# One loop over all 32 experts, and a 4 MB stage for the next expert's down blocks, copied home by GpSimd

## The chip, the core and the metric

The kernel runs on one core of a Trainium2 chip. The metric is the device time of one execution in microseconds; the median of three runs of the kernel before is 1277.75 us. TensorE (PE) multiplies, VectorE (DVE), ScalarE (ACT) and GpSimd (POOL) do the rest, and SyncE (SP) issues the large transfers from HBM.

## The reference, cut to what matters

One layer of a streaming encoder over 320 tokens (256 of a prompt, 64 of a sample), width 1024, in fp32: modulation, a combined projection, stick-breaking attention beside an mLSTM, an output projection, and then a mixture of experts. Only the last part is touched by the change:

```python
logits = h @ w_router + b_router            # h (320, 1024), 32 experts
top_val, top_idx = lax.top_k(logits, 4)
gates = softmax(top_val)
# for each expert e, over the tokens that chose it:
gu = h[tok] @ w_gu[e] + b_gu[e]             # (1024, 2048)
x_glu, x_lin = split(gu); x_glu = min(x_glu, 7); x_lin = clip(x_lin, -7, 7)
act = x_glu * sigmoid(1.702 * x_glu) * (x_lin + 1)
acc[tok] += (act @ w_down[e] + b_down[e]) * gate   # (1024, 1024)
x = x + ga2 * acc
```

Each expert has 8 MB of `w_gu` and 4 MB of `w_down`, so 32 experts are 384 MB that cross from HBM once.

## The kernel before, in words

**Memory.** `ring` has 12 units of 1 MB (128 partitions x 2048 fp32). Before the experts it holds chunks of `w_ada`, `w_in` and `w_out`; then units 0 to 7 hold the eight row blocks of an expert's `w_gu` and units 8 to 11 the four blocks of its `w_down`. `work` is a scratch area that the stages share: first attention and mLSTM, then, from its start on, the expert stage (`h2p`, the tokens in three bf16 parts; `xg`, `actT`, `gc`, `lc`, `sg`, `otok`, `spread`, `pick`, `wpick`, and so on).

**Transfers.** SP issues all weight transfers in program order. The twelve units of expert 0 are issued as the last chunks of `w_ada` and `w_out` are used (L500 to L502). Then a loop over experts 1 to 31 (L509) calls `load_expert`: unit j of expert e waits until PE has used unit j of expert e - 1 (`gu_used` for j below 8, `dn_used` for the others), in the order 0 to 11. After the loop SP stores the output when DVE's last additions are done (`acc_ready`).

**An expert on PE** (`expert`, L1004): read three token counts (this expert's, the one's before, the one's after); wait for `xg`; the bias and blocks 0 to 2 of gate/up (`gate_up`, L907, or L897 and L900 for one size); the first half of the scatter of the expert before (`scatter`, L978); blocks 3 to 5; the second half of that scatter; blocks 6 and 7 and the transposition of the gate weights (`turn_pick`, L968); the gather of the tokens of the next expert (`gather`, L862); the transposition of this expert's activations (`turn_act`, L920); that of the next expert's tokens (`turn_x`, L870); and the down product (`down`, L941), which frees the down units one by one. DVE makes the picks and the gate weights, adds the scattered results to `x` (L1699), clips and multiplies (L1683 to L1690). ACT copies out of PSUM and does the sigmoid.

**Sizes.** Each of these steps exists four times in the code, for up to 32, 64, 96 and 128 tokens (`by_size`: bodies 4, 2, 3, 1); branches pick one by the count of the expert. The shapes 128*32 and 128*64 in a profile row tell 32 and 64 tokens.

**The loop.** `passes` (L420) writes the experts as three pieces of code: expert 0 by itself (nothing before it), a loop for experts 1 to 30, and expert 31 by itself (nothing after it), and then `finish`, which scatters and adds the last expert. Further passes, for experts with over 128 tokens, are skipped by a branch.

**GpSimd** has small work up to the token parts (`h2p`, L1761) and none in the expert stage.

Of the kernel before, what the change touches and what calls it, by code (L numbers as in the profile page):

```python
# [26 lines left out]
P = 128  # L27
# [21 lines left out]
UNITS, GU_UNITS, DN_UNITS, UNIT = 12, 8, 4, 2048  # L49
ADA, WIN, WO = 4, 7, 2  # L50
# [22 lines left out]
for _n, _w in (("ident", P), ("ones", P), ("blk", P), ("tri", P), ("mask_s", 320), ("mask_i", 320), ("sel", MLH * P),  # L73
               ("iota", CAP), ("stack", NE)):
    CONST[_n] = (_at, _at + _w)
    _at += _w
# [22 lines left out]
def build(nc, xT, small, const, b_exp, kcT, vc, c0n, w_ada, w_in, w_out, w_gu, w_down,  # L99
          yT, koT, vo, convo, cno, mo):  # L100
    ctx = ExitStack()
    with ctx:
# [13 lines left out]
        tiny = sb("tiny", [P, 400])  # L116
        modrow = sb("modrow", [P, 4, P])
# [70 lines left out]
        take4, at4 = region(0)  # L188
# [8 lines left out]
        otok = take4(D)  # L197
        spread = take4(T)
        spread_b = take4(T)
        lgT = spread  # L200
        pick = take4(3, CAP, dt=BF16)
        wpick = take4(3, CAP)
        wpick_b = take4(3, CAP)
        xtok = h[:].rearrange("p k t -> p (k t)")[:, 0:D]
        member = take4(3, NE)
        gate = take4(3, NE)
        rank = take4(3, NE)
# [36 lines left out]
        cnti = tn(NE, dt=I32)  # L244
        rows = sb("rows", [P, 4, T])
# [9 lines left out]
        unit_full = [sem(f"unit_full{i}") for i in range(UNITS)]  # L255
        v_chain, a_chain, g_chain = sem("v_chain"), sem("a_chain"), sem("g_chain")
# [137 lines left out]
        def expert_units(e):  # L394

            gu = w_gu.rearrange("o e (k p) n -> (o e) p k n", p=P)
            dn = w_down.rearrange("o e (j p k) n -> (o e) p j k n", p=P, k=2)
            units = [(ring[:, kk, :], gu[e, :, kk, :]) for kk in range(GU_UNITS)]
            units += [(ring[:, GU_UNITS + j, :].rearrange("p (k n) -> p k n", k=2), dn[e, :, j, :, :]) for j in range(DN_UNITS)]
            return units  # L400
# [13 lines left out]
        def used_unit(j, turn):  # L414

            if j < GU_UNITS:
                return gu_used, turn * GU_UNITS + (j + 1)
            return dn_used, turn * DN_UNITS + (j - GU_UNITS + 1)

        def passes(eng, start, expert, finish):  # L420


            eng.wait_ge(cnt_ready, 1)
            start(0, 0, 0)
            expert(0, 0, 0, True, False)
            most = eng.value_load(cmaxi[0:1, 0:1], min_val=0, max_val=T)
            with eng.Fori(1, NE - 1) as e:
                expert(e, e, 0, False, False)
            expert(NE - 1, NE - 1, 0, False, True)
            finish(NE - 1, 0)  # L430
            with eng.Fori(1, PASSES) as b:
                with eng.If(most > b * CAP):
                    start(b * NE, 0, b)
                    expert(b * NE, 0, b, True, False)
                    with eng.Fori(1, NE - 1) as e:
                        expert(b * NE + e, e, b, False, False)
                    expert(b * NE + (NE - 1), NE - 1, b, False, True)
                    finish(b * NE + (NE - 1), b)

        def count(eng, e):  # L440

            return eng.value_load(cnti[0:1, bass.ds(e, 1)], min_val=0, max_val=T)
# [35 lines left out]
        def _(sp):  # L478
# [21 lines left out]
            for j, (dst, src) in enumerate(expert_units(0)):  # L500
                sp.wait_ge(*used_before(PRE + j // 2 - SLOTS))
                sp.dma_start(dst, src).then_inc(unit_full[j], 16)  # L502

            def load_expert(e, turn):
                for j, (dst, src) in enumerate(expert_units(e)):
                    sp.wait_ge(*used_unit(j, turn - 1))
                    sp.dma_start(dst, src).then_inc(unit_full[j], 16)  # L507

            with sp.Fori(1, NE) as e:  # L509
                load_expert(e, e)  # L510
            yv = yT.rearrange("(k p) t -> p k t", p=P)

            def store_y(turn):

                for half in range(2):
                    sp.wait_ge(acc_ready, turn * 8 + 4 * half + 4)
                    sp.dma_start(yv[:, half:KD:2, :], x[:, half:KD:2, :]).then_inc(y_stored, 16)
# [4 lines left out]
            for b in range(1, PASSES):  # L522
                with sp.If(most > b * CAP):
                    with sp.Fori(0, NE) as e:
                        load_expert(e, b * NE + e)
                    store_y(b * NE + (NE - 1))
                    sp.wait_ge(y_stored, b * 32 + 32)
# [9 lines left out]
        def _(pe):  # L537
# [296 lines left out]
            for tt, (t0, n) in enumerate(TILES):  # L834
                last = mm(bank[7][0:n, tt * NE:(tt + 1) * NE], lgT[:, t0:t0 + n], K("stack"), start=True, stop=True)
# [30 lines left out]
            def turn_x(turn, groups):  # L866

                pe.wait_ge(xtok_ready, turn + 1)
# [17 lines left out]
            def up_bias(turn, groups):  # L886
                pe.wait_ge(eh_up_ready, turn + 1)
# [41 lines left out]
            def down_bias(turn, groups):  # L929
                pe.wait_ge(eh_down_ready, turn + 1)  # L930
                if groups in (1, 3):
                    pe.wait_ge(spread_ready, turn + 1)
# [38 lines left out]
            def scatter(i, turn, groups):  # L971
# [8 lines left out]
                for u in range(4):  # L980
                    if i:
                        pe.wait_ge(acc_ready, turn * 8 + (u + 1))
# [7 lines left out]

            def start(turn, e, b):
                n = count(pe, e)
                pe.wait_ge(pick_ready, turn * 3 + 3)
                if not isinstance(b, int):
                    pe.wait_ge(acc_ready, turn * 8)
                by_rows(pe, n, b, lambda groups: (gather(turn, groups), turn_x(turn, groups)))

            def spread_out(i, turn, n, b):
                if i == 0:
                    pe.wait_ge(otok_ready, turn + 1)  # L1000
                    pe.wait_ge(spread_ready, turn + 1)
                by_size(pe, n, b, lambda groups: scatter(i, turn, groups))

            def expert(turn, e, b, begins, ends):  # L1004
                n = count(pe, e)
                before = None if begins else count(pe, e - 1)
                after = None if ends else count(pe, e + 1)
                pe.wait_ge(xg_ready, turn + 1)
                by_size(pe, n, b, lambda groups: (up_bias(turn, groups), gate_up(0, 3, turn, groups)))
# [7 lines left out]
                def last_rows(groups):  # L1017
                    gate_up(6, 8, turn, groups)
                    if not begins:
                        pe.wait_ge(acc_ready, turn * 8)  # L1020
# [3 lines left out]
                if not ends:  # L1024
                    pe.wait_ge(pick_ready, turn * 3 + 6)
                    by_rows(pe, after, b, lambda groups: gather(turn + 1, groups))
                by_size(pe, n, b, lambda groups: (down_bias(turn, groups), turn_act(0, turn, groups), turn_act(1, turn, groups)))
                if not ends:
                    by_rows(pe, after, b, lambda groups: turn_x(turn + 1, groups))
# [14 lines left out]
        def _(act_):  # L1044
# [218 lines left out]

            for i in range(4):
# [15 lines left out]
            def gathered(turn, groups):  # L1280
                act_.wait_ge(gath_ps, turn + 1)
# [6 lines left out]
            def turned(turn, groups):  # L1288

                act_.wait_ge(xtr_ps, turn + 1)  # L1290
# [8 lines left out]
            def start(turn, e, b):  # L1299
                by_rows(act_, count(act_, e), b, lambda groups: (gathered(turn, groups), turned(turn, groups)))  # L1300
# [42 lines left out]
            def expert(turn, e, b, begins, ends):  # L1343
# [3 lines left out]
                if not ends:  # L1347
                    by_rows(act_, after, b, lambda groups: gathered(turn + 1, groups))
                by_size(act_, n, b, lambda groups: activations(turn, groups))
                if not ends:  # L1350
                    by_rows(act_, after, b, lambda groups: turned(turn + 1, groups))
# [8 lines left out]
        def _(v):  # L1360
# [282 lines left out]
            chain(stt(rank[:], bank[5][:, 0:96].rearrange("p (t e) -> p t e", t=3), 1.0, member[:], ALU.add, ALU.mult))  # L1643
            chain(ts(rank[:], rank[:], -1.0, None, ALU.add))
            chain(nc.vector.reduce_max(cmax, bank[5][:, 96:128], AX_X))
            cp(cnti, bank[5][:, 96:128])
# [45 lines left out]
            def add(i, turn):  # L1692
                if i == 0 and not (isinstance(turn, int) and turn == 0):
                    v.wait_ge(acc_ready, turn * 8)
                for u in range(4):
                    v.wait_ge(sc_ps, turn * 8 + (4 * i + u + 1))
# [39 lines left out]
        def _(g):  # L1736
# [20 lines left out]
            for i in range(6):  # L1757
# [4 lines left out]
                                        h2p[0:n, 1, tt, half * 512:half * 512 + 512], ALU.subtract).then_inc(lo_ready, 1)  # L1762

# [5 lines left out]
def constants():  # L1769
# [20 lines left out]
    put("stack", np.tile(np.eye(NE, dtype=np.float32), (P // NE, 1)))  # L1790
# [63 lines left out]
```

## Time and profile before

| | us |
|---|---|
| runs | 1271.48, 1277.75, 1280.69 (median 1277.75) |
| profiled execution | 1283.42, of which the span of the core 1281.6 |
| PE busy | 1108.4 (86% of the span) |
| DVE, ACT, POOL busy | 416.6, 194.3, 44.0 |
| moved | 454.99 MB, mean 355 GB/s |

The profile is of one execution. Its times count from the start of the span. The page cuts the span into 40 slices of 32 us; the rows below take the stretches that matter. "issue" as the cause of an idle time means that the engine waited for nothing that the profile shows.

### The profile page before, as it was taken

What the parts mean: (1) busy time and instruction counts of PE and PEld (TensorE: products, weight loads), DVE (VectorE), ACT (ScalarE), POOL (GpSimd) and SP (SyncE); (2) the same over time, 40 slices, a digit from 0 to 9 for tenths busy, and PEclk for the clock granted to TensorE, in tenths of its full rate; (3) what the DMA queues carried; (4) which work ended last, traced back from release to release, by engine and by line L of the source; (5) the groups of instructions that cost most, each with busy time, mean ns of one, the idle gap of its engine ahead of it and who ended that gap; (6) DMA issues with size and microseconds to landing.
All of it is one profiled execution on the core that took longest, in us unless ns stands there. A gap on an engine that the chain in (4) does not pass through costs nothing.

```text
span 1281.6 us, 21966 instructions
## 1 busy us (share of the span) xinstructions
PE 1108.4 (86%) x7288; PEld 463.7 (36%) x7289; DVE 416.6 (33%) x1295; ACT 194.3 (15%) x427; POOL 44.0 (3%) x27
## 2 busy tenths in 40 slices
PE   4999998976858888679979998999999979869986
PEld 0667664643223223223323332333333323223332
DVE  2133635434215222223233224233223323322233
ACT  2323242122101000011101111011111101101100
POOL 0141110002000000000000000000000000000000
PEclk8998997986979989999999999999999999988988
DMA  9963218730979999999999999999999999999992
GB/s 379 344 232 119 91 68 326 280 131 26 395 313 423 422 422 422 422 422 422 421 422 422 421 423 422 421 422 422 422 422 421 422 422 422 422 422 422 421 421 104
DMA packets 76889, 454.99 MB, mean 355 GB/s; under 512 B 9868, under 2 KB 14732, under 8 KB 24524
## 3 DMA queue, kind: packets, MB, share of 16 engines
q1 hardware_dynamic: 70304, 449.76, 85.6%
q10 hardware_dynamic: 6540, 4.60, 1.3%
q8 instruction: 31, 0.51, 0.2%
q14 instruction: 14, 0.11, 0.0%
HBM read 451.17 MB, written 3.17 MB: 355 GB/s over the span
## 4 chain that ended last, share of the span: by engine, by line
PE 58%; DMA 26%; issue 5%; SPq 5%; DVE 4%; ACT 2%; DVEq 0%; POOL 0%; ACTq 0%
DMA ring<-w_gu 20%; PE psum L907 12%; PE psum L941 11%; PE psum L593 6%; PE psum L900 4%; SPq L507 4%; DMA ring<-w_down 4%; PE psum L978 3%; PE psum L862 3%; PE psum L802 3%; PE psum L897 2%; PE psum L602 2%; DMA ring<-w_ada 2%; PE psum L557 2%; PE psum L870 1%
## 5 line engine op out<-in xcount | busy, mean ns | idle before, releaser
L907 PE MATMUL psum<-ring,work 128*32 128x512 f32 (+1 forms) x1792 | 328.8, 632 | 46.2 <-DMA ring<-w_gu 39.1
L941 PE MATMUL psum<-ring,work 128*32 128x256 f32 (+1 forms) x1760 | 205.8, 470 | 22.5 <-issue 11.2
L1699 DVE SCALAR_TENSOR_TENSOR x<-psum,tiny,x 128x256 f32<-128x256 f32 (+1 forms) x512 | 155.2, 376 | 203.0 <-PE psum L978 203.0
L907 PEld LDWEIGHTS psum<-ring,work 128*32 128x32 f32 (+1 forms) x1792 | 84.1, 126 | 247.1 <-issue 141.1
L1668 DVE TENSOR_SCALAR work<-csb 96x128 bf16<-96x128 f32 x64 | 15.4, 280 | 406.3 <-PE psum L907 337.5
L1050 ACT ACTIVATE work<-psum 128x256 f32<-128x256 f32 (+5 forms) x215 | 88.2, 430 | 336.8 <-PE psum L941 210.7
L941 PEld LDWEIGHTS psum<-ring,work 128*32 128x32 f32 (+1 forms) x1760 | 78.3, 123 | 134.6 <-issue 100.1
L1305 ACT ACTIVATE work<-work 128x128 f32<-128x128 f32 (+2 forms) x64 | 24.2, 378 | 574.3 <-DVE work L1683 574.3
L593 PE MATMUL psum<-h,ring 128*128 128x320 f32 x320 | 91.9, 445 | 1.2 <-ACT h L1085 1.2
L978 PE MATMUL psum<-work 32*128 32x320 f32 (+1 forms) x576 | 79.6, 478 | 4.7 <-issue 3.3
L593 PEld LDWEIGHTS psum<-h,ring 128*128 128x128 f32 x320 | 62.3, 196 | 27.4 <-issue 3.7
L862 PE MATMUL psum<-work 128*32 128x256 bf16 (+4 forms) x846 | 68.2, 320 | 3.7 <-DVE work L1654 3.7
L978 PEld LDWEIGHTS psum<-work 32*128 32x128 f32 (+1 forms) x576 | 36.8, 188 | 68.4 <-issue 57.1
L900 PE MATMUL psum<-ring,work 128*64 128x512 f32 x256 | 57.6, 597 | 0.0
L557 PE MATMUL psum<-ring,cs 128*32 128x512 f32 x192 | 31.0, 775 | 18.4 <-DMA ring<-w_ada 18.4
L890 PE MATMUL psum<-b,work 96*32 96x512 bf16 (+1 forms) x144 | 19.6, 420 | 30.3 <-issue 29.0
L1683 DVE TENSOR_SCALAR work<-psum 128x128 f32<-128x128 f32 (+2 forms) x64 | 23.9, 373 | 62.1 <-PE psum L907 49.4
L862 PEld LDWEIGHTS psum<-work 128*32 128x32 bf16 (+4 forms) x846 | 29.5, 100 | 32.0 <-issue 17.4
L802 PE MATMUL psum<-work,ring 128*128 128x320 f32 x128 | 34.9, 433 | 0.0
L900 PEld LDWEIGHTS psum<-ring,work 128*64 128x64 f32 x256 | 17.3, 137 | 39.8 <-issue 39.8
L897 PE MATMUL psum<-ring,work 128*32 128x512 f32 x256 | 31.6, 626 | 0.0
L1661 DVE TENSOR_SCALAR work<-csb,work 128x128 f32<-128x128 f32 (+1 forms) x108 | 30.0, 338 | 0.0
(213 smaller groups left out, 704.8 us busy)
## 6 DMA issues: line engine op xcount, KB each, us to landing
ring<-w_gu SPq DMA_DIRECT2D x256, 1024.0 KB, 25.7
ring<-w_down SPq DMA_DIRECT2D x128, 1024.0 KB, 23.4
ring<-w_ada SPq DMA_DIRECT2D x12, 2048.0 KB, 9.0
ring<-w_in SPq DMA_DIRECT2D x7, 2048.0 KB, 30.4
ring<-w_out SPq DMA_DIRECT2D x2, 2048.0 KB, 11.1
x<-xT SPq DMA_DIRECT2D x1, 1280.0 KB, 6.0
yT<-x SPq DMA_DIRECT2D x2, 640.0 KB, 4.1
work<-b_exp ACTq DMA_DIRECT2D x3, 384.0 KB, 16.5
```

The costliest lines, as they stand in the source:

```text
L507: sp.dma_start(dst, src).then_inc(unit_full[j], 16)
L557: last = mm(bank[bk][32 * g:32 * g + 32, :], cs[:, kk, :], w[:, u, g * CHC:(g + 1) * CHC], start=kk == 0, stop=kk == KD - 1)
L593: last = mm(bank[t % 2][:, 0:T], w[:, kk, c * P:(c + 1) * P], h[:, kk, :], start=kk == 0, stop=kk == KD - 1)
L802: last = mm(bank[2 + t % 2][:, 0:T], w[:, kk, (t % 4) * P:(t % 4 + 1) * P], mix[:, kk, :], start=kk == 0, stop=kk == KD - 1)
L862: last = mm(o, pick[0:nt, tt, 0:m], h2p[0:nt, part, tt, g * n:(g + 1) * n], start=tt == 0 and part == 0, stop=tt == 2 and part == 2)
L897: mm(o, xg[:, kk, PART_B], cols(ring[:, kk, :]), start=False, stop=kk == KD - 1)
L900: last = mm(o, xg[:, kk, PART_A], cols(ring[:, kk, :]), start=False, stop=kk == KD - 1)
L907: last = mm(o, xg[:, kk, 0:m], cols(ring[:, kk, :]), start=False, stop=kk == KD - 1)
L941: last = mm(o, actT[:, kk, cols], ring[:, GU_UNITS + kk // 2, c1_:c1_ + n], start=False, stop=kk == 7)
L978: return mm(bank[SPREAD_BANKS[u]][:, 0:T], otok[rows_, c0_:c0_ + P], by[rows_, :], start=start, stop=stop)
L1050: return fn(out, in_, ACT.Copy)
L1699: last = stt(x[:, f, cols], bank[SPREAD_BANKS[u]][:, cols], mod[:, 40 + f, sq_:sq_ + 1], x[:, f, cols], ALU.mult, ALU.add)
```

## The change

- `passes` runs all 32 experts in one loop. For expert 0 the "expert before" has a count of zero, its output rows and its spread are set to zero by GpSimd, and its scatter and additions run on zeros; for expert 31 the "expert after" has a count of zero too (column 32 of `stack` and of `rank`), and its picks and its gather run for no token. The semaphores' targets are moved accordingly.
- PE no longer reads three counts at the start of an expert; it reads them into three registers after the first three blocks of the expert before.
- A stage of 4 MB (`stage`, the first 8192 columns of `work`) takes the down blocks of the next expert. SP issues block j of expert e to the stage when the block before it has been copied out (`unit_full[8 + j]`), and GpSimd copies each block to its home in `ring` (`bring_down`) when it has landed (`stage_full`) and PE has used the home's old content (`dn_used`). For expert 0 the down blocks still go home directly.
- The order on SP: gate/up 0, down 0, then (after waits for the mLSTM's end and for the stores of attention and convolution) down 1, gate/up 1, down 2, gate/up 2, and then gate/up e, down e for e from 3 on.
- The tiles of the expert stage move behind the stage in `work`, some into `h` and `rows`; ACT waits for the stores of the mLSTM's state before it writes `h2p`.

```diff
@@ passes
             eng.wait_ge(cnt_ready, 1)
             start(0, 0, 0)
-            expert(0, 0, 0, True, False)
             most = eng.value_load(cmaxi[0:1, 0:1], min_val=0, max_val=T)
-            with eng.Fori(1, NE - 1) as e:
+            with eng.Fori(0, NE) as e:
                 expert(e, e, 0, False, False)
-            expert(NE - 1, NE - 1, 0, False, True)
             finish(NE - 1, 0)
@@ SP
+            def load_gu(e, turn):
+                for j in range(GU_UNITS):
+                    sp.wait_ge(gu_used, (turn - 1) * GU_UNITS + (j + 1))
+                    sp.dma_start(ring[:, j, :], gu_rows[e, :, j, :]).then_inc(unit_full[j], 16)
+
+            def load_dn(e, turn):
+                for j in range(DN_UNITS):
+                    sp.wait_ge(unit_full[GU_UNITS + j], turn * 16)
+                    sp.dma_start(stage[:, j, :].rearrange("p (k n) -> p k n", k=2), dn_rows[e, :, j, :, :]).then_inc(stage_full[j], 16)
...
-            with sp.Fori(1, NE) as e:
-                load_expert(e, e)
+            sp.wait_ge(state_ps, MLH)
+            sp.wait_ge(sb_stored, 16 * 3)
+            sp.wait_ge(conv_stored, 16 * 2)
+            load_dn(1, 1)
+            load_gu(1, 1)
+            load_dn(2, 2)
+            load_gu(2, 2)
+            with sp.Fori(3, NE) as e:
+                load_gu(e, e)
+                load_dn(e, e)
@@ PE
+            counts = [pe.alloc_register(f"count{i}") for i in range(3)]
...
+                if isinstance(b, int):
+                    pe.reg_load(counts, cnti[0:1, 0:3])
...
             def expert(turn, e, b, begins, ends):
-                n = count(pe, e)
-                before = None if begins else count(pe, e - 1)
-                after = None if ends else count(pe, e + 1)
-                pe.wait_ge(xg_ready, turn + 1)
-                by_size(pe, n, b, lambda groups: (up_bias(turn, groups), gate_up(0, 3, turn, groups)))
+                if begins:
+                    before, n, after = None, count(pe, e), count(pe, e + 1)
+                else:
+                    before, n, after = [pe.snap(r) for r in counts]
+                at = ahead(turn, b)
+                pe.wait_ge(xg_ready, at + 1)
+                by_size(pe, n, b, lambda groups: (up_bias(at, groups), gate_up(0, 3, turn, groups)))
+                if not ends:
+                    pe.reg_load(counts, cnti[0:1, bass.ds(e + 1, 3)])
@@ GpSimd
+            g.wait_ge(state_stored, 16 * 2)
+            g.wait_ge(logit_ps, 1)
+            nc.gpsimd.memset(otok[:, 0:256], 0.0).then_inc(otok_ready, 1)
+            nc.gpsimd.memset(spread, 0.0).then_inc(spread_ready, 1)
+
+            def bring_down(turn):
+                for j in range(DN_UNITS):
+                    g.wait_ge(stage_full[j], turn * 16)
+                    g.wait_ge(dn_used, (turn - 1) * DN_UNITS + (j + 1))
+                    nc.gpsimd.tensor_copy(ring[:, GU_UNITS + j, :], stage[:, j, :]).then_inc(unit_full[GU_UNITS + j], 16)
+
+            with g.Fori(1, NE) as e:
+                bring_down(e)
```

## Rows read from the trace of the kernel before

**Rows 1.** The page: GB/s that the DMA engines moved, in 40 slices.
```profile
GB/s 379 344 232 119 91 68 326 280 131 26 395 313 423 422 422 422 422 422 422 421 422 422 421 423 422 421 422 422 422 422 421 422 422 422 422 422 422 421 421 104
```

**Rows 2.** By stretch: us; busy PE, PEld, DVE, ACT, POOL; clock, DMA share, GB/s.
```profile
280.00:300.00 20.00, 10.06 (x59) 7.72 (x59) 13.66 (x47) 11.76 (x24) 5.80 (x6) 0.67 0.08 33
...
340.00:350.00 10.00, 7.16 (x50) 2.24 (x46) 2.33 (x10) 0.60 (x1) 0.00 (x0) 1.00 0.99 385
...
370.00:380.00 10.00, 5.25 (x64) 2.58 (x64) 0.00 (x0) 0.01 (x1) 0.00 (x0) 0.58 0.30 100
...
440.00:1240.00 800.00, 713.71 (x5150) 254.83 (x5146) 246.76 (x854) 90.34 (x224) 0.00 (x0) 0.96 1.01 422
...
1250.00:1260.00 10.00, 8.06 (x40) 2.72 (x36) 5.36 (x16) 1.67 (x5) 0.00 (x0) 0.95 0.41 171
```

**Rows 3.** Timeline of SP's queue: start, length and count of issues.
```profile
257.74 18.03 SPq L502 DMA_DIRECT2D ring<-w_down  x4
316.99 12.48 SPq L507 DMA_DIRECT2D ring<-w_gu  x8
337.94 5.46 SPq L507 DMA_DIRECT2D ring<-w_down  x4
346.42 17.06 SPq L507 DMA_DIRECT2D ring<-w_gu  x8
376.90 3.83 SPq L507 DMA_DIRECT2D ring<-w_down  x4
```

**Rows 4.** Timeline of PE in experts 0 to 2; idle before it in brackets.
```profile
312.32 1.06 PE L890 MATMUL psum<-b,work 96*64 96x512 bf16 x4 [1.30 <-ACT work L1050]
...
334.25 8.65 PE L941 MATMUL psum<-ring,work 128*64 128x512 f32 x32 [0.98 <-issue]
344.93 0.40 PE L890 MATMUL psum<-b,work 96*32 96x512 bf16 x4 [2.02 <-issue]
...
368.90 0.69 PE L870 MATMUL psum<-csb,h 128*128 128x128 f32 x2 [3.38 <-issue]
374.75 5.44 PE L941 MATMUL psum<-ring,work 128*32 128x256 f32 x64 [5.16 <-issue]
382.10 0.40 PE L890 MATMUL psum<-b,work 96*32 96x512 bf16 x4 [1.91 <-issue]
...
400.50 0.40 PE L890 MATMUL psum<-b,work 96*32 96x512 bf16 x4 [1.85 <-issue]
```

**Rows 5.** DMA queue of instructions before 382 us and after 1235 us: packets, MB; between, none.
```profile
q8 instruction: 22, 0.36, 0.4%
...
q8 instruction: 9, 0.15, 1.2%
```

**Rows 6.** Timeline of PE in the last experts, and one of 64 tokens at 1079.
```profile
1079.73 0.61 PE L890 MATMUL psum<-b,work 96*64 96x512 bf16 x4
...
1102.53 7.09 PE L941 MATMUL psum<-ring,work 128*64 128x512 f32 x32 [0.17 <-issue]
1109.54 0.40 PE L890 MATMUL psum<-b,work 96*32 96x512 bf16 x4
...
1150.70 1.94 PE L907 MATMUL psum<-ring,work 128*32 128x512 f32 x8 [1.42 <-DMA ring<-w_gu]
...
1169.39 0.95 PE L890 MATMUL psum<-b,work 96*32 96x512 bf16 x8 [1.74 <-issue]
...
1232.58 0.62 PE L890 MATMUL psum<-b,work 96*64 96x512 bf16 x4 [0.62 <-issue]
...
1243.74 7.87 PE L907 MATMUL psum<-ring,work 128*64 128x512 f32 x23 [3.54 <-issue]
...
1260.22 9.87 PE L941 MATMUL psum<-ring,work 128*64 128x512 f32 x32 [0.47 <-ACT work L1050]
```

**Rows 7.** POOL by line and shape: busy us, mean ns of one.
```profile
L1740 POOL CAST b<-work 96x3072 bf16<-96x3072 f32 x1 | 2.7, 2741 | 57.7 <-DMA work<-b_exp 57.7
...
L1761 POOL TENSOR_TENSOR work<-work 128x512 bf16<-128x512 f32 x4 | 4.5, 1152 | 61.1 <-ACT work L1050 61.1
```

More of the change, by code:

```diff
@@ L116, in build @@
         tiny = sb("tiny", [P, 400])
+        rows = sb("rows", [P, 4, T])
         modrow = sb("modrow", [P, 4, P])
@@ L186, in build @@
         sq = mix
-        take4, at4 = region(0)
+        stage = work[:, 0:STAGE].rearrange("p (j n) -> p j n", j=DN_UNITS)
+        take4, at4 = region(STAGE)
         h2p = take4(3, 3, D, dt=BF16)
@@ L196, in build @@
         res = work[:, res_at:res_at + 3 * 512].rearrange("p (a n) -> p a n", a=3)
-        otok = take4(D)
         spread = take4(T)
-        spread_b = take4(T)
         lgT = spread
         pick = take4(3, CAP, dt=BF16)
-        wpick = take4(3, CAP)
-        wpick_b = take4(3, CAP)
-        xtok = h[:].rearrange("p k t -> p (k t)")[:, 0:D]
+        hflat = h[:].rearrange("p k t -> p (k t)")
+        xtok = hflat[:, 0:D]
+        otok = hflat[:, D:2 * D]
+        rflat = rows[:].rearrange("p a t -> p (a t)")
+        wpick, wpick_b = [rflat[:, i * 3 * CAP:(i + 1) * 3 * CAP].rearrange("p (t n) -> p t n", t=3) for i in range(2)]
+        spread_b = rflat[:, 6 * CAP:6 * CAP + T]
         member = take4(3, NE)
         gate = take4(3, NE)
-        rank = take4(3, NE)
+        rank = take4(3, NE + 1)
         lg = take4(3, NE)
@@ L255, in build @@
         unit_full = [sem(f"unit_full{i}") for i in range(UNITS)]
+        stage_full = [sem(f"stage_full{i}") for i in range(DN_UNITS)]
         v_chain, a_chain, g_chain = sem("v_chain"), sem("a_chain"), sem("g_chain")
@@ L392, in halves @@
             return slice(0, n), slice(n, 2 * n)
[L394 to L400, printed above, removed]
+        gu_rows = w_gu.rearrange("o e (k p) n -> (o e) p k n", p=P)
+        dn_rows = w_down.rearrange("o e (j p k) n -> (o e) p j k n", p=P, k=2)
         def used_before(n):
@@ L834, in _ @@
             for tt, (t0, n) in enumerate(TILES):
-                last = mm(bank[7][0:n, tt * NE:(tt + 1) * NE], lgT[:, t0:t0 + n], K("stack"), start=True, stop=True)
+                last = mm(bank[7][0:n, tt * NE:(tt + 1) * NE], lgT[:, t0:t0 + n], K("stack")[:, 0:NE], start=True, stop=True)
             last.then_inc(logit_ps, 1)
@@ L1692, in add @@
             def add(i, turn):
-                if i == 0 and not (isinstance(turn, int) and turn == 0):
-                    v.wait_ge(acc_ready, turn * 8)
+                if i == 0:
+                    v.wait_ge(acc_ready, turn * 8 + 16)
                 for u in range(4):
-                    v.wait_ge(sc_ps, turn * 8 + (4 * i + u + 1))
+                    v.wait_ge(sc_ps, turn * 8 + (4 * i + u + 9))
                     f = FEATURES[4 * i + u]
@@ L1762, in _ @@
                                         h2p[0:n, 1, tt, half * 512:half * 512 + 512], ALU.subtract).then_inc(lo_ready, 1)
+            g.wait_ge(state_stored, 16 * 2)
[3 more added lines that the diff above has]
+            def bring_down(turn):
+                for j in range(DN_UNITS):
+                    g.wait_ge(stage_full[j], turn * 16)
[3 more added lines that the diff above has]
+                bring_down(e)
+            g.wait_ge(cnt_ready, 1)
+            most = g.value_load(cmaxi[0:1, 0:1], min_val=0, max_val=T)
+            for b in range(1, PASSES):
+                with g.If(most > b * CAP):
+                    with g.Fori(0, NE) as e:
+                        bring_down(b * NE + e)
 _OUTS = (("yT", (D, T)), ("koT", (512, T)), ("vo", (T, 512)), ("convo", (D, 2, 3)), ("cno", (2, MLH, P, VN)),
```

86 lines of the change are left out of this document (44 added, 42 removed).

## The prediction

> **What bounds the kernel now.** I read four views. First the page's slices [rows 1]: from slice 12 on the transfers run at 421 to 423 GB/s without a dip, whatever the size of the expert. The long stretch [rows 2] gives 422 over 800 us with PE busy 713.71 of them. So the expert stage is bound by HBM traffic: a unit of 1 MB takes 1.0486 MB / 422 GB/s = 2.485 us, an expert 29.8 us. What can change the time is how early this stream becomes continuous, how many units it still has to carry then, and what follows its last unit.
>
> Second, the start of the stream. The down blocks of expert 0 are issued until 275.8 [rows 3], then there is nothing to fetch: 33 GB/s between 280 and 300 [rows 2]. The stream starts at 317.0, when PE uses the first unit of expert 0, is slightly thin between 340 and 350 (385 GB/s) and nearly stops between 370 and 380 (100 GB/s) [rows 2]. The reason stands in SP's queue: gate/up 2 is issued by 363.5, the next thing, down 2, waits for PE's down product of expert 1, and goes out at 376.90 [rows 3]. That product came late because PE stood still for 3.38 and 5.16 us with the cause "issue" [rows 4]. From 376.90 the stream has 4 + 29 x 12 = 352 units left: 874.7 us. 376.90 + 874.7 = 1251.6; the windows say that the last bytes land at 1254.0 (171 GB/s over the ten us from 1250 is 4.0 us of full rate) [rows 2]. The model misses 2.4 us, which is the way of a transfer.
>
> Third, the end. The last time that PE waits for weights is at 1150.70, gate/up of expert 28; from there to the end it waits for none [rows 6]. It finishes its last down product at 1270.1 (1260.22 + 9.87), 16 us after the last unit landed, and the scatter, the additions and the store take the 11.5 us that are left. So the end belongs to PE, but PE's clock of 1150.70 is set by the stream: both the stream and the last four experts on PE carry through to the time.
>
> **Part 1, down blocks of expert 1 in the stage.** SP's new waits (mLSTM done, stores landed) are behind its issue at 275.8, and what stands behind them in its queue is gate/up 1, which can't go before 317 anyway. Four units, 9.9 us of transfer, fit into the idle 40 us before 317 and leave the stream. That they are issued at 276 to 280 delays nobody.
>
> **Part 2, the hole at 370.** The new order is gate/up 1, down 2, gate/up 2, gate/up 3. Down 2 needs the copy of down 1 out of the stage, which needs expert 0's down product. That product frees its first unit at 337.94 [rows 3]. To it come the zero scatter of expert 0 (two times 0.8 us of PE, about 1.6), the copy (1.83 us, below) and c, the stalls of a loop entered for the first time. The stream is then continuous if PE reaches expert 2 before down 2 and gate/up 2 have been moved, 12 x 2.485 = 29.8 us later. Expert 1 takes 18.4 us when the loop's code has run once (382.10 to 400.50), against 37.2 the first time (344.93 to 382.10) [rows 4]. In the changed kernel expert 0 has run the loop, so expert 1 should need about 18.4: expert 2 starts some 5 us before the stream runs dry, and the hole closes. Why the second time is fast: the queue that brings instructions has 22 packets before 382 us and 9 after 1235 us, and none in the 853 us between [rows 5]; the whole loop, all four sizes, stays in place once it was fetched.
>
> The Trainium skill, Runtime: NRT & Kernel Launch, Instruction fetch mechanics, says that an engine has no instruction cache, only a window refilled in order, with 2048 instructions for PE, and that a taken branch outside of it stalls for a fetch. By this rule one loop would stall as often as three pieces of code if the body were larger than the window; the trace speaks for a body that fits, since nothing is fetched between 382 and 1235.
>
> The size of c. Before, expert 1 lost 37.2 - 18.4 = 18.8 us; 1.1 of it is a larger scatter, so 17.7 are stalls. Expert 0, whose code was cold too, took 312.3 to 344.9, 32.6 us [rows 4]; a warm expert of that size takes 29.8 with 2.7 us of scatter [rows 6], so 5.5 us are more than warm. Its down product alone took 8.65 for 7.09, a matter of the clock; with as much for its gate/up some 2.5 are clock and 3 are stalls. The loop's first round is entered from straight code as expert 0's was, but has branches more, and runs while the stream is full from 317 on as expert 1's did. I take c = 5 beyond what expert 0 had, nearer to expert 0's row because size and place in time are its own; bounds 0 and 15.
>
> Down 2 goes out at 337.9 + 1.6 + 1.8 + 5 = 346.4 with 360 units left: 894.6 us, plus 2.4: the last unit lands at 1243.4 instead of 1254.0. Parts 1 and 2 together: **10.6 us earlier** (c = 0: 15.6; c = 15: 0.6).
>
> **Part 3, the copies.** 124 copies of 128x2048 fp32. No row shows this form. The nearest is GpSimd's cast of 96x3072, 2741 ns, 0.89 ns a column: 1.83 us. The upper bound is its two-input operation, 1152 ns for 512 columns: 4.6 us. The cast and the two-input row both stand in [rows 7]. Four copies are 7.3 (18.4) us of an expert's 29.8, so GpSimd doesn't become the bound. A copy delays a block for PE by 1.83 us, but only the down product waits, and PE catches up; and when SP waits for a copy before it issues the next block to the stage, the eight units of a gate/up are still queued (20 us of stream). At the very end the last unit lands at 1243.4, is copied by 1245.2 and multiplied by 1247; PE gets there later (below). Cost taken as 1 us for the down products that meet a late copy in the last experts; bounds 0 and 4.
>
> **Part 4, the last experts on PE.** Expert 31 (64 tokens) took 1232.58 to 1270.1, 37.5 us. The same size in the loop took 1079.73 to 1109.6, 29.9, and 1.1 less with the smaller scatter: 28.8 [rows 6]. The difference of 8.7 us is above all a stall of 3.54 at 1240 and slower products after it (9.87 us of down products for 7.09). In one loop both go, and the empty gather (1.3 us of PE) lies beside DVE's gating, for which PE waits anyhow. Reading the counts early takes up to 1.74 us of "issue" at the start of an expert, 0 where the queue of products is long [rows 6]; two of the four last experts show it: 2 us. Against it stands that `finish` is now entered from the loop, and its code has to be fetched: 3 to 5 us by the stalls of PE in the first round [rows 4], hidden in part by the last down product; and that full clock at the end is not sure (2.8). I take 8.7 + 2 - 3.5 - 1.4 = **5.8 us** earlier; bounds 0 and 10.7.
>
> **The sum.** Profiled execution: 10.6 + 5.8 - 1 = 15.4 us less, span 1266, execution 1268. The profiled execution (1283.42) stands 5.7 above the median of the runs, so the same 15.4 off 1277.75 gives **1262.3**. Runs of this kernel differ by 0.7%, so 1%, 12.8 us, is about what a measurement tells from no change.
>
> **Rivals.**
> (A) The first round of the loop pays what expert 1 paid before (c = 15, or expert 1 stays slow through other sizes' code). For it: expert 0 has 64 tokens and expert 1 32, other bodies of the same steps, and the full stream makes each fetch slow. Against it: from expert 2 on other sizes come too, and nothing is fetched [rows 5]. The hole then moves ahead of down 2 instead of closing: 0.6 + 5.8 - 1 = 5.4 us gained, 1272.
> (B) Slower: GpSimd's copies read and write 1 MB for every third unit that lands, and the transfers into the same memory lose rate. Price: each per cent off 422 GB/s costs 9 us over 360 units. From 1.7% the gain is gone, from 3.1% (409 GB/s) it is slower by over 1%; with 3.5% off, 31.5 - 15.4 = 16 us more than before, 1294. Nothing in the trace has GpSimd and a stream of 8 KB rows at the same time, so it can't be excluded.
> (C) DVE waits for GpSimd. Where PE is behind the stream, copies start with the down product and end in the next gate/up, where DVE has slack; where PE waits for the stream, a copy falls on DVE's clip and multiply of an expert, four operations of two inputs, 1.8 us each at worst. For the four last experts 7.3 us: 1269.
> The Trainium skill, SBUF — State Buffer, SBUF: two separate sides, speaks on both: engine ports and DMA ports can't contend, which is against (B), and GpSimd and VectorE share one port pair as an exclusive lock against VectorE operations with two SBUF inputs, which is (C). No row of the kernel before shows either.
> (D) The stage isn't filled in the idle time, because a wait ahead of down 1 ends late; then parts 1 and 2 fail and only part 4 less the copies is left, 4.8 us: 1273. Against it: the last of what it waits for is the mLSTM, which comes before the output projection, and it is the output projection that frees the units of down 0, issued until 275.8 [rows 3].
>
> **How the numbers follow.** Forecast 0.64, (A) 0.14, (B) 0.12, (C) 0.07, (D) 0.03. The forecast's own range is 1252 to 1272: 1252.5 is c = 0 with the whole of part 4 (15.6 + 10.7 - 1 off 1277.75), 1272 is c = 10 with nearly nothing of part 4. The range for 8 in 10 goes from 1250 to 1280, which takes in (A), (C), (D) and the part of (B) up to 2% of lost rate. Faster by over 1% (under 1265): 0.54, most of the forecast (0.52) and a little of (C). Within 1%: 0.34, the rest of the forecast (0.12), (A), (D), most of (C). Slower by over 1%: 0.12, (B).
>
> **What the profile after would show.** Right: about 40 us before PE's first expert, down blocks of expert 1 landing in the stage; no slice under 415 GB/s from 350 us on; expert 1 on PE in 18 to 20 us; last unit landing near 1243; copies of 1.8 us; no instruction packets between the first round and the end; expert 31 in 29 us. Wrong: a hole ahead of down 2 of over 10 us (A); a long stretch below 415 GB/s (B); L1687 and L1690 longer or later behind clips (C). A cold `finish` of more than 5 us would eat part 4.

## The result: 22.5% slower, and what the profile after shows

| | us |
|---|---|
| before, median of 4 runs | 1279.16 (1271.48 to 1280.69) |
| changed, median of 4 runs | 1563.57 (1559.49 to 1573.53) |
| ratio, 95% interval | 1.225 [1.217, 1.233] |
| span of the profiled execution | 1281.6 before, 1564.5 after |

I had forecast 1262 with a range of 1250 to 1280. Four lines of the page of the changed kernel already hold the answer: the GB/s in 40 slices (39 us each here), the queue that brings instructions (packets, MB, share), and two of the costliest groups.

```profile
GB/s 379 348 120 109 94 368 168 138 313 231 380 394 282 370 340 411 310 260 411 380 269 223 268 376 321 271 354 322 271 278 324 325 322 326 325 342 321 310 323 37
...
q8 instruction: 217, 3.56, 1.0%
...
L1803 POOL COPY ring<-work 128x2048 f32<-128x2048 f32 x124 | 234.7, 1895 | 998.0 <-DMA work<-w_down 730.2
...
L906 PE MATMUL psum<-b,work 96*32 96x512 bf16 (+1 forms) x144 | 29.7, 563 | 178.9 <-issue 177.3
```

The stream that ran at 421 to 423 GB/s [rows 1] now swings between 223 and 411. The row of the copies gives them no blame: 1895 ns each, close to the 1.83 us of the forecast, and GpSimd is 18% busy. But 217 packets of instructions came instead of 31, and PE stood idle for 177 us before the bias products (L906), the first products of an expert, with the cause "issue". The waits of PE, first in the changed kernel, then for the same three steps in the kernel before (us in total, times, longest):

```profile
PE psum L906 <- issue: 177.3, 26, 12.3
PE psum L957 <- issue: 89.2, 38, 5.0
PE psum L923 <- issue: 38.1, 21, 3.6
```

```profile
PE psum L890 <- issue: 29.0, 16, 2.2
PE psum L941 <- issue: 11.2, 24, 5.2
...
PE psum L907 <- issue: 5.7, 3, 3.5
```

The three sum to 305 us, where the kernel before had 46: 259 us more, against 283 by which the span grew. Beside that PE is busy 68 us longer (1176.5 for 1108.4), and no longer waits the 49 us that the kernel before waited for `w_gu` and `w_down`: among the eight longest of PE's waits none is for them any more. The timeline of PE shows how it looks in an expert of the changed kernel; the number in brackets is the idle time before:

```profile
1078.81 1.06 PE L906 MATMUL psum<-b,work 96*64 96x512 bf16 x4 [8.77 <-issue]
1079.66 7.12 PE L923 MATMUL psum<-ring,work 128*64 128x512 f32 x24
...
1107.03 8.79 PE L957 MATMUL psum<-ring,work 128*64 128x512 f32 x32 [3.37 <-issue]
1123.20 1.07 PE L906 MATMUL psum<-b,work 96*64 96x512 bf16 x4 [7.39 <-issue]
```

One round of 64 tokens takes 44.4 us (1078.81 to 1123.20), where the kernel before needed 29.8 [rows 6] (1 us of the difference is a larger gather). About 7 to 9 us are lost at the start of the round and 3 to 5 ahead of the down product, the same places at which the kernel before stood still in its first round [rows 4]. And fetching goes on all the time: of the queue's packets, 79 fall between 500 and 1000 us, where the kernel before had none [rows 5]. By stretch (us; busy PE, PEld, DVE, ACT, POOL; granted clock, DMA share, GB/s):

```profile
440.00:1500.00 1060.00, 776.12 (x5052) 277.76 (x5059) 261.58 (x860) 122.75 (x244) 204.68 (x108) 0.86 0.80 320
```

320 GB/s for 422, and a granted clock of 0.86 for 0.96 [rows 2], in a stretch in which PE is busy 73% of the time for 89%. The down product above took 8.79 us for 7.09.

So the loop's code, which stayed in place before, seems to be fetched again in every round. Which part of the change does that? The loop didn't grow. Counted in the compiled program, PE's loop has 1681 instructions before and 1671 after. What moved is where it starts: at instruction 4127 before, at 2680 after, since the code of expert 0 ahead of it is gone. A packet of that queue is 16 KB (0.51 MB in 31), and an instruction has 64 bytes in the compiled program, so a packet holds 256. 4127 is 31 into a block of 256, 2680 is 120 into one. That is theory 1: the loop stays only if it touches no more than seven blocks (1792 instructions). By this count alone the changed loop would just fit (120 + 1671 = 1791); the theory adds that a few instructions, which the compiled program doesn't hold, stand ahead of it and push the loop into the eighth block. Theory 2: the form of the one loop (its zero expert, the counts read into registers) breaks it. Theory 3: the stage and its copies do.

### The profile page after: what moved, and what is told of

Read it like the earlier page. It is cut to its first block, busy times and chain, and to the rows that moved or that the text cites. A ratio compares the mean times of both kernels' runs of the same rounds, so it can differ in the third digit from the quotient of the medians.

```text
span 1564.5 us, 22228 instructions
## 1 busy us (share of the span) xinstructions
PE 1176.5 (75%) x7338; PEld 490.6 (31%) x7343; DVE 442.8 (28%) x1318; ACT 235.0 (15%) x460; POOL 279.0 (18%) x153
## 4 chain that ended last, share of the span: by engine, by line
PE 69%; issue 22%; DVE 5%; ACT 2%; DMA 2%; DVEq 0%; SPq 0%; POOL 0%; ACTq 0%
PE psum L923 20%; PE psum L957 15%; PE psum L609 5%; PE psum L994 4%; PE psum L878 4%; PE psum L916 4%; PE psum L913 2%; PE psum L818 2%; DVE x L1729 2%; PE psum L618 2%; PE psum L906 2%; DMA ring<-w_ada 2%; PE psum L886 1%; PE psum L573 1%; PE psum L984 1%
## 5 line engine op out<-in xcount | busy, mean ns | idle before, releaser
L1803 POOL COPY ring<-work 128x2048 f32<-128x2048 f32 x124 | 234.7, 1895 | 998.0 <-DMA work<-w_down 730.2
L923 PE MATMUL psum<-ring,work 128*32 128x512 f32 (+1 forms) x1792 | 356.2, 688 | 38.1 <-issue 38.1
L957 PE MATMUL psum<-ring,work 128*32 128x256 f32 (+1 forms) x1760 | 236.0, 526 | 89.2 <-issue 89.2
L923 PEld LDWEIGHTS psum<-ring,work 128*32 128x32 f32 (+1 forms) x1792 | 98.0, 138 | 251.9 <-issue 249.2
L906 PE MATMUL psum<-b,work 96*32 96x512 bf16 (+1 forms) x144 | 29.7, 563 | 178.9 <-issue 177.3
L957 PEld LDWEIGHTS psum<-ring,work 128*32 128x32 f32 (+1 forms) x1760 | 90.0, 137 | 219.9 <-issue 207.5
L1076 ACT ACTIVATE work<-psum 128x256 f32<-128x256 f32 (+8 forms) x176 | 70.2, 419 | 133.8 <-PE psum L609 56.2
L1076 ACT ACTIVATE h<-psum 128x256 f32<-128x256 f32 (+2 forms) x69 | 35.0, 513 | 354.3 <-PE psum L957 308.0
L994 PE MATMUL psum<-work,h 64*128 64x320 f32 (+1 forms) x528 | 76.3, 470 | 1.4 <-ACT h L1076 1.1
L878 PE MATMUL psum<-work 128*32 128x256 bf16 (+5 forms) x878 | 67.4, 316 | 5.0 <-DVE work L1684 4.3
L906 PEld LDWEIGHTS psum<-b,work 96*32 96x32 bf16 (+1 forms) x144 | 6.3, 115 | 202.1 <-issue 201.8
L916 PE MATMUL psum<-ring,work 128*64 128x512 f32 x256 | 57.6, 597 | 0.0
L994 PEld LDWEIGHTS psum<-work,h 64*128 64x128 f32 (+1 forms) x528 | 35.7, 187 | 67.6 <-issue 53.8
L573 PE MATMUL psum<-ring,cs 128*32 128x512 f32 x192 | 28.8, 726 | 17.8 <-DMA ring<-w_ada 17.8
```

The costliest lines, as they stand in the source:

```text
L573: last = mm(bank[bk][32 * g:32 * g + 32, :], cs[:, kk, :], w[:, u, g * CHC:(g + 1) * CHC], start=kk == 0, stop=kk == KD - 1)
L878: last = mm(o, pick[0:nt, tt, 0:m], h2p[0:nt, part, tt, g * n:(g + 1) * n], start=tt == 0 and part == 0, stop=tt == 2 and part == 2)
L916: last = mm(o, xg[:, kk, PART_A], cols(ring[:, kk, :]), start=False, stop=kk == KD - 1)
L923: last = mm(o, xg[:, kk, 0:m], cols(ring[:, kk, :]), start=False, stop=kk == KD - 1)
L957: last = mm(o, actT[:, kk, cols], ring[:, GU_UNITS + kk // 2, c1_:c1_ + n], start=False, stop=kk == 7)
L994: return mm(bank[SPREAD_BANKS[u]][:, 0:T], otok[rows_, c0_:c0_ + P], by[rows_, :], start=start, stop=stop)
```

## The experiments

### Moving the loop, and nothing else

Ahead of PE's loop a branch that is never taken now jumps over matrix products that never run.

```diff
+            if pad:                       # PE alone
+                with eng.If(most > 2 * CAP):
+                    for _ in range(pad):  # 36 in the changed kernel, 30 in the one before
+                        nc.tensor.matmul(bank[7][:, 0:T], ones, x[:, 0, :], start=True, stop=True)
             with eng.Fori(0, NE) as e:
```

> The changed kernel with 145 instructions that never run put ahead of TensorE's expert loop, nothing else; the loop then starts 9 instructions into a block of 256 instead of 120. Theory 1 (position): the loop's 1671 instructions stay in place only if they touch seven blocks of 256; started at 120 plus the few that the runtime puts ahead they touch eight, and a part is fetched again in every round. Then this kernel has about 30 packets of instructions instead of 217 and takes 1250 to 1272 us, as I had forecast. Theory 2 (one loop, with its zero expert and its register loads, is itself what breaks the fetching): 1563 as before. Theory 3 (the copies or the stage slow it down): 1563.

Measured: 1268.62 us (10 runs, 1265.57 to 1274.42), ratio to before 0.9963 [0.9940, 0.9986]. From 22.5% slower to 0.4% faster by 145 instructions that never run. The page of the shifted kernel:

```profile
GB/s 376 335 244 112 113 67 332 283 215 52 270 406 421 422 422 422 422 422 422 422 422 421 422 422 422 422 422 422 422 422 422 422 422 422 422 422 422 422 422 164
...
q8 instruction: 20, 0.33, 0.1%
```

All parts of the change are in this kernel, so theories 2 and 3 fall as causes of the 22.5%.

> The kernel BEFORE with 121 instructions that never run ahead of TensorE's loop, so that the loop starts 152 into a block of 256 instead of 31 and touches eight blocks. Theory 1: some 200 packets of instructions and 1500 us or more, though nothing of the change is in it. Theories 2 and 3: 1279, about 31 packets.

Measured: 1725.82 us in one run. Its page:

```profile
span 1723.9 us, 21967 instructions
...
q8 instruction: 292, 4.78, 1.2%
```

The kernel before, with none of the change in it, becomes 35% slower than it was (1275.03 beside it) when its loop is moved. That is the same cause from the other side.

### Shortening the loop where it lies

```diff
@@ by_size, on PE: no expert here has over 96 tokens, so the body never ran
                 with eng.If(n > b * CAP + CAP // 2):
-                    with eng.If(n > b * CAP + CAP * 3 // 4):
-                        body(1)
-                    with eng.Else():
-                        body(3)
+                    body(3)
```

> The changed kernel at its own place (loop starts at 120), but without the bodies for 97 to 128 tokens on TensorE, which no expert here runs: the loop is 1385 instructions instead of 1671 and touches six or seven blocks wherever it lies. The work that runs is the same. Theory 1: 1250 to 1275 us and about 30 packets. Theories 2 and 3: 1563.

Measured: 1268.78 us in one run, and on its page:

```profile
span 1267.0 us, 22204 instructions
...
q8 instruction: 20, 0.33, 0.1%
```

At its own bad place the loop stays when it is 1385 instructions long. It isn't the place alone, then, but the blocks that place and length together touch.

### Where the edge is

> The changed kernel with 233 instructions that never run ahead of the loop: it starts 97 into a block, and ends 24 before the end of the seventh. Counted in the compiled program alone both this and the changed kernel (120) would touch seven blocks; the changed kernel is slow, so something ahead shifts the count. If that shift is under 24 instructions, this one is fast (1268, some 20 packets); if it is larger, slow (over 1500, some 200 packets).

Measured: 1567.51 us, 218 packets. Slow, so more than 24 instructions stand ahead.

> The changed kernel with its loop starting 61 instructions into a block (97 was slow, 9 fast; the kernel before lies at 31). Where the edge lies tells how many instructions the runtime puts ahead: the loop ends at 61 + 1671 = 1732 of the 1792 of seven blocks. Fast (1268, some 20 packets) if fewer than 60 stand ahead, slow (1565, some 217 packets) if more. If place mattered by something other than a count of blocks, a time in between is possible.

Measured: 1541.91 us, 202 packets. Slow again, so more than 60.

> The changed kernel with its loop starting at 153, the place at which the shifted kernel before took 1726 us with 292 packets. If the place alone sets how much is fetched again, this one has more packets than the changed kernel's 217, near 292, and about 1700 us. If the two kernels' loops differ in what they fetch (one loop or three pieces, counts read early), it stays near 217 packets and 1565.

Measured: 1713.54 us, 300 packets. Close to the 1725.82 us and 292 packets of the kernel before at this place.

Together, with three kernels of the next two sections (one run each, but medians for the shifted kernel, the one before, the changed one and those three):

| kernel | loop starts in its block at | length | packets | us |
|---|---|---|---|---|
| shifted | 9 | 1671 | 20 | 1268.62 |
| before | 31 | 1681 | 31 | 1275.03 |
| at 61 | 61 | 1671 | 202 | 1541.91 |
| edge | 97 | 1671 | 218 | 1567.51 |
| changed | 120 | 1671 | 217 | 1563.57 |
| shorter | 120 | 1385 | 20 | 1268.78 |
| three pieces with stage | 32 | 1671 | 31 | 1274.83 |
| one loop, no stage | 9 | 1671 | 20 | 1270.10 |
| stage for two experts | 9 | 1671 | 20 | 1262.58 |
| at 153 | 153 | 1671 | 300 | 1713.54 |
| before, shifted | 152 | 1681 | 292 | 1725.82 |

If seven blocks is the limit, the kernel before says 31 + 1681 + d <= 1792, so d, the instructions ahead, is at most 80, and the one at 61 says that d is over 60. Every row fits a d between 61 and 80; I didn't count d itself. So that place and length decide is shown by the runs; that they do so by a count of seven blocks is the rule that fits all eleven rows. The count doesn't tell how much is fetched: about six packets a round from 61 to 120 and nine at 152 and 153, and why is open.

The Trainium skill, Runtime: NRT & Kernel Launch, Instruction fetch mechanics, gives PE an instruction memory of 2048 instructions, refilled in blocks of 256, and says that a taken branch to a target outside of the current window of two pages waits for a fetch. The packets of 16 KB agree with the blocks, and a loop of 1681 instructions that needs no fetch agrees with the 2048. It doesn't agree with a window of two such blocks, which would be 512 instructions. And 2048 instructions would be eight blocks, where here seven stay and eight don't: the measurement decides. That the eighth is taken up by the block fetched ahead is a guess; no run here shows it.

### Which part of the change is worth what, with the loop in a good place

```diff
@@ stage and copies, three pieces of code as before
             start(0, 0, 0)
+            expert(0, 0, 0, True, False)
...
-            with eng.Fori(0, NE) as e:
+            with eng.Fori(1, NE - 1) as e:
                 expert(e, e, 0, False, False)
+            expert(NE - 1, NE - 1, 0, False, True)
```

> The changed kernel with the stage and the copies, but experts 0 and 31 written out beside the loop again; TensorE's loop starts 32 into a block, as before. Theory 1: no refetching, and the stage's part alone, 5 to 12 us under before: 1267 to 1275. Theory 2: the same. Theory 3: 1500 or more, since all copies are in it.

Measured: 1274.83 us (10 runs), ratio 0.9993 [0.9968, 1.0017]: no difference, at the upper end of what I expected. Yet its last unit lands at 1244.3 (181 GB/s over the ten us from 1240), ten us before that of the first profile, and its profiled span is 1271.6 for 1281.6. About 1 us of the gap between the two comparisons lies outside of the span: its runs take 2.7 to 3.2 us more than their span, all others 1.8 to 1.9. Its PE in expert 31:

```profile
1234.89 5.18 PE L929 MATMUL psum<-ring,work 128*64 128x512 f32 x16 [2.33 <-issue]
...
1248.78 1.50 PE L942 MATMUL psum<-csb,work 128*128 128x128 f32 x4 [2.92 <-DVE work L1726]
1250.75 9.21 PE L963 MATMUL psum<-ring,work 128*64 128x512 f32 x32 [0.47 <-ACT work L1082]
```

The stall of expert 31, whose code is run for the first time, is still there (2.33), the down product is slow (9.21 for 7.09), and ahead of it PE waits 2.92 us for VectorE, where the kernel before waited 1.40 and 0.29 in both of its profiles.

```diff
@@ one loop, no stage (loop at 9)
-                    sp.wait_ge(unit_full[GU_UNITS + j], turn * 16)
-                    sp.dma_start(stage[:, j, :]...).then_inc(stage_full[j], 16)
+                    sp.wait_ge(dn_used, (turn - 1) * DN_UNITS + (j + 1))
+                    sp.dma_start(ring[:, GU_UNITS + j, :]...).then_inc(unit_full[GU_UNITS + j], 16)
...
-            with g.Fori(1, NE) as e:
-                bring_down(e)
```

> One loop, no stage and no copies: down blocks go straight to their home and wait for the down product before, in the order gate/up e, down e. The loop starts 9 into a block, as in the shifted kernel of the first call. My forecast's parts 2 and 4 without part 1: the hole ahead of down 2 goes, since expert 1 runs warm code, 364 units are left, and the last experts gain 5.8 us: 8 to 12 us under a profile of before, 1264 to 1270. Rival (the copies hold VectorE up and cost what the stage gives): then this one is as fast as the shifted kernel or faster, and VectorE's busy time is 40 us lower.

Measured: 1270.10 us (12 runs), ratio 0.9961 [0.9946, 0.9976]. That is just above the 1264 to 1270 that I expected, and the rival's condition holds in time (as fast as the shifted kernel) and in VectorE's busy time, 423.0 us for 481.5. The profile of this kernel from 1250, by stretch as above:

```profile
1250.00:1260.00 10.00, 8.60 (x42) 3.00 (x40) 0.43 (x2) 0.98 (x2) 0.00 (x0) 1.00 0.18 70
```

The last unit lands at 1251.7, 7.5 us later than with the stage. So the stage does bring its time at the start, and in the medians all of it is lost behind.

> The kernel before itself, to see how its profile and its runs scatter. The first profile (1283.4 us) was at the slow end of its runs. If the scatter comes from instruction fetches and the clock in the first two experts and in expert 31, this profile is nearer 1275, with less idle time before the down product of expert 1 or in expert 31. Ratio 1.00.

Measured: 1277.76 us (10 runs), ratio 1.0002 [0.9981, 1.0024]. The profiled execution took 1280.24 (span 1278.4), not nearer to 1275 as I had expected, and stands at the upper end of the runs again. Its stall ahead of the down product of expert 1 is shorter (3.38 for 5.16). Its stall in expert 31 is the same 3.55 us; its down product ran at full clock:

```profile
1244.35 7.06 PE L907 MATMUL psum<-ring,work 128*64 128x512 f32 x23 [3.55 <-issue]
...
1258.06 0.51 PE L920 MATMUL psum<-csb,work 128*128 128x128 f32 x2 [1.40 <-DVE work L1690]
...
1259.84 7.09 PE L941 MATMUL psum<-ring,work 128*64 128x512 f32 x32 [0.47 <-ACT work L1050]
```

So 2.8 us of the first profile [rows 6] were a lower clock that isn't there in every execution (the three pieces with the stage had it too, 9.21), and I had counted half of them as the change's to win.

### What the copies cost, and a version that is faster than both

The stage for the down blocks of experts 1 and 2 alone; from expert 3 on they go home directly.

```diff
             load_dn(1, 1)
             load_gu(1, 1)
             load_dn(2, 2)
             load_gu(2, 2)
             with sp.Fori(3, NE) as e:
                 load_gu(e, e)
-                load_dn(e, e)
+                load_home(e, e)      # waits for dn_used of e - 1, writes to ring
...
-            with g.Fori(1, NE) as e:
-                bring_down(e)
+            bring_down(1)
+            bring_down(2)
```

> The shifted kernel, with the stage used for the down blocks of experts 1 and 2 alone; from expert 3 on they go home directly and GpSimd is idle. The start of the stream is the same, so the last unit lands at 1244 as in the shifted kernel. If VectorE's waits for GpSimd cost time only in the last expert (3.3 us seen before its transpositions), this one ends 2 to 5 us earlier: 1262 to 1267. If the waits cost nothing: 1268, as the shifted kernel.

Measured: 1262.58 us (6 runs, 1261.76 to 1265.53), ratio 0.9901 [0.9879, 0.9924], 1.0% under the kernel before and apart from the shifted kernel's 0.9963 [0.9940, 0.9986]. It is 7.5 us under the kernel without a stage (1270.10), which is what the stage brings at the start: the last unit lands 7.2 us earlier. Against the shifted kernel the stream is the same to 0.3 us. By stretch, first the shifted kernel, then this one:

```profile
440.00:1200.00 760.00, 684.18 (x4847) 244.24 (x4843) 285.05 (x812) 116.90 (x232) 192.13 (x101) 0.95 1.01 422
...
1240.00:1250.00 10.00, 7.13 (x59) 3.05 (x59) 5.12 (x8) 2.61 (x7) 5.74 (x3) 0.83 0.43 178
```

```profile
1240.00:1250.00 10.00, 9.00 (x75) 3.87 (x75) 2.76 (x8) 2.62 (x7) 0.00 (x0) 1.00 0.46 190
```

What differs is VectorE and, at the end, PE's clock. The timeline of the shifted kernel in expert 31, where GpSimd copies blocks as they land and VectorE multiplies out the gates; L1721 and L1724 are L1687 and L1690 of the kernel before:

```profile
1240.54 1.90 POOL L1807 COPY ring<-work 128x2048 f32<-128x2048 f32 x1 [0.58 <-DMA work<-w_down]
...
1241.80 0.91 DVE L1721 SCALAR_TENSOR_TENSOR work<-work 128x256 f32<-128x256 f32 x1
...
1243.01 1.91 POOL L1807 COPY ring<-work 128x2048 f32<-128x2048 f32 x1 [0.58 <-DMA work<-w_down]
1243.08 2.11 DVE L1721 SCALAR_TENSOR_TENSOR work<-work 128x256 f32<-128x256 f32 x1
...
1245.23 0.42 DVE L1724 TENSOR_TENSOR work<-work 128x256 f32<-128x256 f32 x1
...
1245.71 0.65 PE L940 MATMUL psum<-csb,work 128*128 128x128 f32 x2 [1.98 <-DVE work L1724]
...
1247.17 8.13 PE L961 MATMUL psum<-ring,work 128*64 128x512 f32 x32
```

The same steps of PE in the kernel with the stage for two experts:

```profile
1242.88 0.50 PE L945 MATMUL psum<-csb,work 128*128 128x128 f32 x2 [0.29 <-DVE work L1729]
...
1244.34 7.09 PE L966 MATMUL psum<-ring,work 128*64 128x512 f32 x32 [0.17 <-issue]
```

The second L1721 starts 0.07 us after a copy has begun and ends 0.27 us after the copy does: 2.11 us for an operation of 0.42. The first, 0.91 us long, also ends 0.27 us after the copy beside which it ran. Over the whole run, by line and shape (busy us, mean ns), the shifted kernel and then the one with the stage for two experts:

```profile
L1721 DVE SCALAR_TENSOR_TENSOR work<-work 128x256 f32<-128x256 f32 x30 | 32.1, 1069 | 0.0
```

```profile
L1726 DVE SCALAR_TENSOR_TENSOR work<-work 128x256 f32<-128x256 f32 x30 | 12.5, 416 | 0.0
```

The operations with two inputs in SBUF wait for a copy to end; one with a single input, in PSUM (L1717, 419 ns a piece before, 418 in the shifted kernel), doesn't. The Trainium skill, SBUF — State Buffer, SBUF: two separate sides, says just this (an exclusive lock on the port pair that GpSimd and VectorE share, against VectorE operations with two SBUF inputs while GpSimd reads SBUF), and the trace agrees, 2.11 us for 0.42. Its other half, that engines and transfers don't contend, agrees too: 422 GB/s over 760 us with 101 copies in them.

PE waited 34.1 us in 33 places for L1724 in the shifted kernel, and 4.8 us for the same step in the kernel with the stage for two experts. Most of that lies where PE waits for the stream anyhow (30.8 us for `w_gu` in the shifted kernel, 57.6 in the other); the 2.7 us in expert 31, for 0.5 in the other, don't. The down product behind them took 8.13 us for 7.09, with a granted clock of 0.83 for 1.00 in these ten us. Together that is the 3.2 us by which expert 31 is shorter. The profiles differ by 3.9 us and the medians by 6.0; what the other two are, no profile here shows.

## Why the prediction was wrong

**The step that failed** is in part 2: "the whole loop, all four sizes, stays in place once it was fetched". The rows showed that for the loop before at its place [rows 5], and I carried it to a loop at another place. In the changed kernel the loop did not stay: 79 packets of instructions in 500 us where I had none, and 259 us more of waits with the cause "issue". I had weighed the size of the body only, and didn't ask where it begins. By the rule of seven blocks the loop ended just inside the seventh before, and taking the code of expert 0 away moved it into the eighth; 145 instructions that never run put it back, and 1268.62 us came. Of my rivals none had it. (A) was nearest, since it charged the cold code, but once: 17.7 us. The changed kernel pays 7 to 9 and 3 to 5 us in most rounds. And no row that I had could have told the cost of a loop that doesn't stay, so the range of 1250 to 1280 had no place for it.

**With the loop in a good place most steps held** against the profile of before, in part because errors cancel. For each: forecast, then the shifted kernel.
- Down 2 issued at 346.4: 347.17. This is closer than I had earned. The same sum, counted from where expert 0 began, gives c = 7.1 for my 5 (stalls of 1.62 and 5.90 us in expert 0, where the kernel before had 0.98), and expert 0 began 1.4 us earlier (310.95 for 312.32), which no term of mine had.
- Expert 1 in 18.4 us: 17.0 (350.18 to 367.16). The hole at 370 is gone: 406 GB/s in the slice that holds it and 421 in the next.
- Last unit at 1243.4: 1244.2. The stage's four units are out of the stream.
- Copies of 1.83 us: 1.90. They don't slow the transfers, so rival (B) is out. So is (D): the stage's first blocks were issued from 273.4 to 280.0.
- Expert 31 in 28.8 us: 31.0 (1224.26 to 1255.3), and 27.8 in the kernel with the stage for two (1223.62 to 1251.4). The 2.7 us of waits for VectorE in it are rival (C), which I had given 0.07 and a price of 7.3 us. It acts, part 3 had not charged it, and the medians of the two kernels differ by 6.0 us.
- `finish` entered cold, 3.5 us: nothing. From the end of the last down product to the end of the span it is 11.6 us, for 11.5 before. That makes up for the 2.2 us that expert 31 was too long.
- Span 1266: 1266.9.

The stall and the length of expert 1 in the timeline of PE:

```profile
341.59 8.65 PE L961 MATMUL psum<-ring,work 128*64 128x512 f32 x32 [5.90 <-issue]
350.18 0.40 PE L910 MATMUL psum<-b,work 96*32 96x512 bf16 x4
...
367.16 0.41 PE L910 MATMUL psum<-b,work 96*32 96x512 bf16 x4
```

**The size, median to median, was still too large.** 14.7 us less between two profiles, but only 0.37% (4.7 us) between the medians, 1275.03 beside 1268.62 being 6.4. The two profiles of the kernel before give executions of 1283.42 and 1280.24, at the upper end of its runs (1269.44 to 1283.88), while the profile of the shifted kernel is at its median. I took the profiled execution's excess of 5.7 us as a constant that stands on both sides; it stands on one. Part of it is the clock in expert 31 (2.8 us in one profile, 0 in the other). What its faster executions do otherwise is open; none of them was profiled.

## What to carry to other kernels

For a large loop it can matter more than all the change saves whether its code stays with the engine, and that hangs on where the loop begins and how long it is: after a change that adds or takes away code ahead of a large loop, look at the instruction queue's packets in the steady stretch first, and if there are any, move the loop or shorten it before judging the change. A copy on GpSimd isn't free because GpSimd is idle: ask which VectorE operations read two SBUF inputs meanwhile; here a stage used for two experts kept the whole gain at the start and paid for none of the other 116 copies.

## What the runs showed of the hardware that I had not expected

- A loop of 1671 instructions on PE took 1268.62 us or 1541.91 to 1713.54 us, by its place alone, while the same kernel with a loop of 1385 took 1268.78 at a place that is slow for the longer one.
- How much is fetched again also depends on the place: 202 to 218 packets from 61 to 120, 292 to 300 at 152 and 153 (one profile each).
- With one loop, ACT loads its table in every round instead of once (the kernel in three pieces with the stage loads it once too). It isn't in the chain that ended last, 1.28 us a time. The page of the changed kernel:

```profile
L1332 ACT ACT_TABLE_LOAD x32 | 41.1, 1283 | 43.3 <-issue 43.3
```
